# Value projection of two dilated attention groups: one 512-column product over half-depth weight units

## The reference, cut to what matters

```
h = rmsnorm(x, norm1_w) * (1 + scale1) + shift1
gq, gk, gv, gr, g_lr, aq, ak, av, merge_a, merge_b = split(h @ w_in)
# ATTN_GROUPS = ((128, 1), (512, 4), (2048, 16)), 4 heads of 64 in each group
# v = av: [512 tokens, 3 groups x 4 heads x 64]
# group 1 attends within blocks of 128 neighbouring tokens,
# groups 2 and 3 over tokens that are 4 and 16 apart
```

## Time and profile before

| | |
|---|---|
| median of 3 runs | 1018.53 us (1017.75 to 1021.41) |
| profiled execution, span from the first to the last instruction (no other time of it is given) | 1023.4 us |
| PE busy | 977.9 us, 96% |
| DVE / ACT / POOL busy | 516.0 / 374.7 / 95.1 us |
| mean granted PE clock | 0.954 |
| data moved | 112.69 MB, 110 GB/s |

### The profile page before, as it was taken

How to read it: one execution, slowest core, us unless ns; L and a number is a source line. 1 busy time by engine, 2 the same in 40 slices (tenths; PEclk the granted TensorE clock), 3 DMA queues, 4 the chain that set the end, 5 groups by cost and what they waited for, 6 DMA issues and landing times.

```text
span 1023.4 us, 12197 instructions
## 1 busy us (share of the span) xinstructions
PE 977.9 (96%) x4755; PEld 822.0 (80%) x4755; DVE 516.0 (50%) x639; ACT 374.7 (37%) x461; POOL 95.1 (9%) x66
## 2 busy tenths in 40 slices
PE   3699999999999999999999999799999999999996
PEld 2589888886998888888888887688888888888885
DVE  5981367264566555655315433755555545623323
ACT  5343110152763433552522233533433333423225
POOL 3710131110000000000001222100000000000003
PEclk8589997696999999999999999999999999999999
DMA  9833373360435212122222262133233242232202
GB/s 341 308 117 95 105 234 109 106 211 16 129 119 165 83 42 83 43 83 71 77 99 83 83 206 83 41 99 107 82 106 99 82 115 90 85 121 82 104 19 82
DMA packets 115040, 112.69 MB, mean 110 GB/s; under 512 B 4516, under 2 KB 106278, under 8 KB 112695
## 3 DMA queue, kind: packets, MB, share of 16 engines
q1 hardware_dynamic: 114279, 109.96, 33.7%
q10 hardware_dynamic: 720, 2.16, 0.6%
HBM read 104.77 MB, written 4.19 MB: 106 GB/s over the span
## 4 chain that ended last, share of the span: by engine, by line
PE 90%; DVE 5%; DMA 1%; issue 1%; SPq 1%; ACT 1%; POOL 0%; DVEq 0%; ACTq 0%; POOLq 0%
PE bank L1443 26%; PE bank L1444 25%; PE bank L1445 25%; DVE ada_in L935 2%; PE bank L1640 2%; PE bank L1550 2%; PE bank L1820 1%; DMA ada_in<-in_ada_w_dram 1%; PE bank L1525 1%; PE bank L1561 1%; PE bank L1627 1%; PE bank L1661 1%; PE bank L1586 1%; PE bank L1545 1%; DVE h_lo L1371 1%
## 5 line engine op out<-in xcount | busy, mean ns | idle before, releaser
L1443 PE MATMUL bank<-h_hi,w_hi 128*128 128x512 f32 (+1 forms) x696 | 280.3, 403 | 1.8 <-DVE rope_t L1026 0.8
L1444 PE MATMUL bank<-h_lo,w_hi 128*128 128x512 f32 (+1 forms) x696 | 274.9, 395 | 0.0
L1445 PE MATMUL bank<-h_hi,w_lo 128*128 128x512 f32 (+1 forms) x696 | 274.6, 395 | 0.0
L1443 PEld LDWEIGHTS bank<-h_hi,w_hi 128*128 128x128 f32 (+1 forms) x696 | 132.4, 190 | 30.9 <-issue 2.5
L1445 PEld LDWEIGHTS bank<-h_hi,w_lo 128*128 128x128 f32 (+1 forms) x696 | 132.2, 190 | 29.0
L1444 PEld LDWEIGHTS bank<-h_lo,w_hi 128*128 128x128 f32 (+1 forms) x696 | 132.2, 190 | 27.5 <-issue 0.2
L969 DVE TENSOR_TENSOR w_lo<-raw,w_hi 128x2048 fp32r<-128x2048 f32 (+3 forms) x48 | 88.2, 1849 | 76.3 <-ACT w_hi L553 76.3
L976 DVE TENSOR_TENSOR w_lo<-raw,w_hi 128x2048 fp32r<-128x2048 f32 x32 | 73.4, 2292 | 91.7 <-ACT w_hi L561 91.7
L1397 DVE SCALAR_TENSOR_TENSOR conv<-bank,vecs,conv 128x511 f32<-128x511 f32 x88 | 65.7, 748 | 67.4 <-ACT conv L864 61.9
L553 ACT ACTIVATE w_hi<-raw 128x2048 fp32r<-128x2048 f32 (+2 forms) x45 | 73.4, 1644 | 69.2 <-DMA raw<-in_w_in_dram 60.3
L561 ACT ACTIVATE w_hi<-raw 128x2048 fp32r<-128x2048 f32 x33 | 62.9, 1905 | 72.2 <-PE bank L1445 72.2
(11 more groups left out here) (233 smaller groups left out, 1328.2 us busy)
## 6 DMA issues: line engine op xcount, KB each, us to landing
raw<-in_w_up_dram SPq DMA_DIRECT2D x44, 512.0 KB, 4.9
raw<-in_w_in_dram SPq DMA_DIRECT2D x19, 1024.0 KB, 5.3
raw<-in_ada_w_dram SPq DMA_DIRECT2D x16, 1024.0 KB, 5.6
raw<-in_w_down_dram SPq DMA_DIRECT2D x22, 512.0 KB, 3.6
raw<-in_w_in_dram SPq DMA_DIRECT2D x20, 512.0 KB, 5.1
ada_in<-in_ada_w_dram SPq DMA_DIRECT2D x16, 512.0 KB, 7.9
raw<-in_w_gla_branch_dram SPq DMA_DIRECT2D x4, 1024.0 KB, 5.0
raw<-in_w_out_dram SPq DMA_DIRECT2D x4, 1024.0 KB, 5.0
```

What stands on the lines that cost most here:

```text
L1443: pe.matmul(out_ap, wh, xh, start=first, stop=False, skip_group_check=True)
L1444: pe.matmul(out_ap, wh, xl, start=False, stop=False, skip_group_check=True)
L1445: return pe.matmul(out_ap, wl, xh, start=False, stop=last, skip_group_check=True)
```

## The change

The last two value units are no longer cut by group but by depth: unit `vw` 0 holds depth tiles 0 to 3 of the 512 columns of groups two and three, unit `vw` 1 depth tiles 4 to 7. For each residue r, the 128 tokens are the stationary operand, and all 512 columns stream into a bank of its own, `side[1 + r]` (banks 3 to 6). The first half leaves its sums open there (`vw_half`), and the second ends them, residue by residue (`vw_ready`). ACT copies residues 0 and 2 to `v_ext`, DVE residues 1 and 3. The scores wait for these copies, since they write the same banks. The `v` units of groups two and three no longer take tiles of banks 0 and 1.

```diff
-UNITS = ([("v", g, 0) for g in range(GROUPS)]
+UNITS = ([("v", 0, 0), ("vw", 0, 0), ("vw", 1, 0)]
...
-    return {"lr": 1, "wa": 8}.get(unit[0], 2)
+    return {"lr": 1, "wa": 8, "vw": 0}.get(unit[0], 2)
...
+        def multiplied(eng, n):
+
+            if UNITS[n][0] == "vw":
+                eng.wait_ge(vw_half if UNITS[n][1] == 0 else vw_ready, 1 if UNITS[n][1] == 0 else NB)
+            else:
+                eng.wait_ge(acc_ready, last_tile(n) + 1)
...
+                elif kind == "vw":
+                    sp.dma_start(raw[:, slot, :].rearrange("p (k n) -> p k n", k=KT // 2),
+                                 w_in_v[:, a * KT // 2:(a + 1) * KT // 2, COL_AV + UW:COL_AV + 3 * UW]).then_inc(done, 16)
...
                 if n >= 2:
-                    act.wait_ge(acc_ready, last_tile(n - 2) + 1)
+                    multiplied(act, n - 2)
...
+            def evac_wide():
+
+                for r in range(0, NB, 2):
+                    act.wait_ge(vw_ready, r + 1)
+                    v = side[1 + r][:, :].rearrange("p (g h n) -> p g h n", g=2, h=HEADS)
+                    for hd in range(2):
+                        act.activation(v_ext[:, r, 1:3, hd::2, hd * DH:(hd + 1) * DH], v[:, :, hd::2, :],
+                                       ACT.Copy).then_inc(vw_act, 1)
...
-            for g in range(GROUPS):
-                n = UNIT[("v", g, 0)]
-                if g > 0:
+            for n in range(GROUPS):
+                if n > 0:
                     split_hi(n + 1)
-                for t in range(2):
-                    evac(n, t)
-                if g == 1:
+                if n == 0:
+                    for t in range(2):
+                        evac(n, t)
+                if n == 2:
+                    evac_wide()
+                if n == 1:
...
+            def evac_wide():
+
+                dve.wait_ge(spilled, 16)
+                dve.wait_ge(nt_done, KT)
+                dve.wait_ge(hh_done, KT)
+                for r in range(1, NB, 2):
+                    dve.wait_ge(vw_ready, r + 1)
+                    v = side[1 + r][:, :].rearrange("p (g h n) -> p g h n", g=2, h=HEADS)
+                    for hd in range(2):
+                        dve.tensor_copy(v_ext[:, r, 1:3, hd::2, hd * DH:(hd + 1) * DH],
+                                        v[:, :, hd::2, :]).then_inc(vw_dve, 1)
...
+            evac_wide()
             dve.wait_ge(rot_act, 3)
...
-                        tok = slice(blk * P, (blk + 1) * P) if kind == "gv" or a == 0 else slice(blk, SEQ, DIL)
+                        tok = slice(blk * P, (blk + 1) * P)
...
+            def wide_values(half):
+
+                n = UNIT[("vw", half, 0)]
+                pe.wait_ge(raw_used, RAW_AT[("w", n)] + 1)
+                for r in range(NB):
+                    for j in range(KT // 2):
+                        k = half * KT // 2 + j
+                        w = tuple(v[:, n % 2, 2 * j * UW:2 * (j + 1) * UW] for v in (w_hi, w_lo))
+                        s = tuple(v[:, k, r::DIL] for v in (h_hi, h_lo))
+                        last = three(side[1 + r][:, :], s, w, k == 0, k == KT - 1)
+                    if half == 1:
+                        last.then_inc(vw_ready, 1)
+                if half == 0:
+                    last.then_inc(vw_half, 1)
...
+                if hh == 0:
+                    pe.wait_ge(vw_act, NB)
+                    pe.wait_ge(vw_dve, NB)
...
-                    evacuated(pe, (("v", GROUPS - 1, 0), 0))
-                    evacuated(pe, (("v", GROUPS - 1, 0), 1))
+                    evacuated(pe, (("v", 0, 0), 0))
+                    evacuated(pe, (("v", 0, 0), 1))
...
-            for n in range(1, GROUPS):
-                for t in range(2):
-                    product(n, t)
+            for half in range(2):
+                wide_values(half)
```

More of the change, by code:

```diff
@@ L270, in hybrid_block_kernel @@
         v_ones = sem("v_ones")
+        vw_half, vw_ready, vw_act, vw_dve = (sem(n) for n in ("vw_half", "vw_ready", "vw_act", "vw_dve"))
         rope_sum, qk_in = sem("rope_sum"), [sem(f"qk_in{i}") for i in range(2)]
```

## The result

The kernel after takes **994.5 us** (median of 4 runs, 992.75 to 996.7) against 1018.14 us for the kernel before in the same comparison. The ratio is 0.9767 with a 95% interval of 0.9736 to 0.9797. Repeated twice beside other kernels it gave 0.9775 (0.9754 to 0.9796) and 0.9777 (0.9749 to 0.9805). The forecast was 995.8 us in 990.5 to 1003, faster at 0.94.

What follows compares the result with a forecast made beforehand. TensorE (PE) was taken to bound the kernel, busy 977.9 of 1023.4 us. Matmuls -22.4 and start -0.35 sum to -22.8, the rest 0; from the median 1018.5 that gives 995.8 us, own range 991 to 1001, judged against 990.5 to 1003.

Steps and rivals of the forecast that it cites:

- What bounds the stretch: Value matmuls of groups two and three: strided weight load sets 0.234 us per start, streaming of 0.107 to 0.12 beside it.
- Does it hide under 512 columns: Wide value matmuls: load and streaming run side by side, 0.234 us each (bounds 0.227 to 0.341); 96 take 22.5 us, net -22.4.
- rows 6: Profile rows of score matmuls with strided weights, 128 columns: 0.231 us each at clock 1.00, 0.221 at clock 0.50.
- Rows 7: Profile rows of records of the same streaming size with neighbouring weights: 1.87 / 16 = 0.117 us at clock 1.00.
- Start: First matmul of the stage no longer waits for the copy of group one out of bank 0: -0.35 us.
- Weight units: Units cut by depth: first query/key unit ready at 84.9, PE asks at 87.1, so 0 with 2.2 us in hand.
- Sine block, copies, shuffles: ScalarE's sines move up to 70 to 74.4 us, half its copies go to VectorE, SP's shuffles follow PE: all 0.
- Sum: Whole kernel: -22.4 - 0.35 = -22.8 us, taken from the median 1018.5, giving 995.8 us.
- A: Wide matmuls: load and streaming one after the other, 0.341 us per matmul, 1006.0 us in all; chance 0.07.
- D: Change does nothing (compiler cuts 512 columns in two, or both loads remain): 192 loads at 0.234, 1018 us; chance 0.01.
- C: First query/key unit late, PE waits at 87 us, clock stays down over six units: 1054 us; chance 0.02.
- B: Behind the stage, PE's half-clock stretches lie otherwise and give back the gain: 1013 to 1023 us; chance 0.04.

Runs made afterwards that it cites:

- The first experiment: Kernel before, but groups two and three load 128 neighbouring tokens as weights instead of every fourth: 995.27 us, ratio 0.9768.
- the second experiment: Kernel before, but depth tiles 1 to 6 of groups two and three stream 128 columns instead of 256: 1017.88 us, ratio 1.0003.
- the late unit: Kernel after, but ScalarE copies its two residues out before it splits the first query/key unit: 997.09 us, ratio 0.9786.

## Why the prediction was right

- *What bounds the stretch.* Right: the strided weight load, 0.234 us, with the streaming hidden beside it. The first experiment shows that the stride is the cause, the second that the streaming is hidden.
- *Does it hide under 512 columns.* Right, and rows 6 pointed to it: a pace that stays at 0.22 to 0.23 while the clock changes by two. Rows 7, which the forecast took for the streaming time of such a record, cannot tell streaming from a plain load, so its "0.21 to 0.23 us" at half clock was an assumption; the second experiment holds the same comparison with the streaming known, at both clocks. The choice of 0.234 was low by 0.003: 0.2367, so 22.7 us at the pace and 22.91 with the slower first step, against 22.5. Why the two together cost a little more than either was not tried.
- *The two rules of the Trainium skill's "TensorE: Matmul & The Clock Gate".* Section "The mechanism" has it that a load overlaps only with matmuls of other row groups, section "LDWEIGHTS (loading the stationary operand)" that its time depends on the column count alone: by the runs both fail here. 128, 256 and 512 columns all start within 0.234 to 0.237 us of each other, all on the full 128 rows, and the same 128 columns of weights give a pace of 0.12 or 0.234 us by their stride. (The first of these sections also speaks of a background weight buffer for such loads, which the runs do not contradict.)
- *Start.* 0.35 forecast, 0.56 measured.
- *Weight units.* Right that nothing waits; 3.6 us in hand instead of 2.2, since the unit landed at 78.1 and not at 80.5. The forecast took the end of all transfers for the end of this one, on the safe side. The unit after it was ready at 95.4 us (96.3 forecast).
- *Sine block, copies, shuffles.* All at 0, as forecast; DVE's pairs of copies took 0.75 us each (0.7 forecast).
- *Sum.* -22.8 forecast. Between the medians it is 23.6, of which the stage and its head give 22.6; the other 1.0 is inside the interval of the ratio (about 21 to 27 us).
- *Rivals.* A fell with the second experiment (the rows of 256 columns at half clock and of 128 at full clock, not its time), D with the 96 records of 512 columns, C with the late unit. Of B the premise held: the stretch behind the stage varies by 8.6 us between profiles. The sum was not given back.

## What to carry to other kernels

Compare matmuls by the distance between their starts, and group them by how the stationary operand is addressed: if half the columns do not cost less, the weight load is the limit. Then either stream more columns for each load, as here, or have an engine with time to spare write the operand in the order in which it is loaded, as for the scores. A row of the same load at another clock tells whether load and streaming run side by side, before anything is built. Look at the granted clock of an experiment before its time is read: here a rival would have given the same time by way of the clock.

## What was not expected of the hardware

A stride of two floats in the stationary operand costs next to nothing (0.12 us from start to start, a load record of 0.20 us against 0.19), a stride of four doubles the pace (0.234, a record of 0.33). The load keeps that pace when the clock is halved. And a PE that is busy without a gap can lose its clock: with most matmuls behind strided loads cut from 256 to 128 columns, at the same 0.234 us from start to start, the granted clock went from 1.00 to 0.50 for over 40 us, and the time did not change, since the load set the pace.
